# Gather, scatter and their place in the expert loop of a two-layer decoder step

## The reference, cut to what matters

```python
logits = (h @ w_router) + b_router
top_v, top_i = lax.top_k(logits, 2)
top_w = softmax(top_v)
combine = sum(one_hot(top_i, 8) * top_w[..., None], axis=-2)
for e in range(8):
    g, u = split(h @ w_gu[e], 2)          # 1024 -> 2 x 3584
    out += combine[:, e:e+1] * ((silu(g) * u) @ w_down[e])   # 3584 -> 1024
```

## Time and profile before

| what | value |
|---|---|
| three runs | 2363.34, 2367.22, 2367.55 us |
| median | 2367.22 us |
| span of the profiled execution | 2364.9 us (the page gives no other time of it) |
| TensorE busy | 2150.8 us, 91% |
| VectorE busy | 1484.2 us, 63% |
| ScalarE busy | 1091.4 us, 46% |
| mean granted TensorE clock | 0.944 of full |
| read from memory | 533.32 MB, 230 GB/s over the span |

### The profile page before, as it was taken

The page is one execution under the profiler, slowest core; times in us unless marked ns, Lnnn a source line. Parts: engine busy times, 40 slices in busy tenths (PEclk is TensorE's granted clock), DMA queues, the critical chain, the costliest instruction groups (busy, mean ns, idle before and its releaser), DMA issues.

```text
span 2364.9 us, 29561 instructions
## 1 busy us (share of the span) xinstructions
PE 2150.8 (91%) x10775; PEld 1662.0 (70%) x10775; DVE 1484.2 (63%) x1684; ACT 1091.4 (46%) x961; POOL 14.9 (1%) x26
## 2 busy tenths in 40 slices
PE   5989899869877899998978999999999999999995
PEld 2443355545656699997966878788787878788783
DVE  5980220267331444535567979788887979788885
ACT  4740020024220233333324757676676757676672
POOL 0000100000000000000000000000000000000000
PEclk9999999957988999998987999999999999999997
DMA  9984333200354564453425979899797979899790
GB/s 320 386 296 110 116 111 114 83 1 1 114 157 121 223 240 160 164 174 110 143 73 176 371 288 368 317 329 373 283 368 284 367 289 373 313 329 373 279 371 25
DMA packets 262788, 537.62 MB, mean 227 GB/s; under 512 B 14876, under 2 KB 56068, under 8 KB 262438
## 3 DMA queue, kind: packets, MB, share of 16 engines
q1 hardware_dynamic: 258514, 520.34, 62.6%
q0 software_dynamic: 1984, 13.45, 1.7%
q10 hardware_dynamic: 2196, 2.61, 0.3%
HBM read 533.32 MB, written 11.35 MB: 230 GB/s over the span
## 4 chain that ended last, share of the span: by engine, by line
PE 85%; DVE 9%; ACT 3%; issue 2%; DMA 1%; ACTq 1%; DVEq 0%; POOL 0%; PEldq 0%
PE ps L1358 23%; PE ps L1846 13%; PE ps L1825 9%; PE ps L1827 9%; PE ps L1826 9%; PE ps L1684 5%; PE ps L1686 5%; PE ps L1685 5%; DVE alo L798 2%; PE ps L1574 1%; PE ps L1486 1%; DMA ring<-in_w_ada 1%; PE ps L1809 1%; ACT ahi L593 1%; PE ps L1589 1%
## 5 line engine op out<-in xcount | busy, mean ns | idle before, releaser
L1307 DVE TENSOR_TENSOR wlo<-ring,whi 128x2048 fp32r<-128x2048 f32 x336 | 767.1, 2290 | 118.0 <-ACT whi L757 118.0
L757 ACT ACTIVATE whi<-ring 128x2048 fp32r<-128x2048 f32 x336 | 642.1, 1918 | 232.9 <-PE ps L1827 166.3
L1825 PE MATMUL ps<-whi,XTh 128*128 128x512 f32 x896 | 355.2, 396 | 0.0
L1827 PE MATMUL ps<-whi,XTl 128*128 128x512 f32 x896 | 350.0, 391 | 0.0
L1826 PE MATMUL ps<-wlo,XTh 128*128 128x512 f32 x896 | 349.3, 390 | 0.0
L1825 PEld LDWEIGHTS ps<-whi,XTh 128*128 128x128 f32 x896 | 168.6, 188 | 36.1 <-DVE wlo L1307 2.5
L1827 PEld LDWEIGHTS ps<-whi,XTl 128*128 128x128 f32 x896 | 168.5, 188 | 36.0
L1826 PEld LDWEIGHTS ps<-wlo,XTh 128*128 128x128 f32 x896 | 168.8, 188 | 33.5
L1150 DVE TENSOR_TENSOR flo<-ring,fhi 128x2048 fp32r<-128x2048 f32 x42 | 96.3, 2292 | 137.4 <-ACT fhi L600 137.4
L600 ACT ACTIVATE fhi<-ring 128x2048 fp32r<-128x2048 f32 x42 | 80.6, 1920 | 174.0 <-PE ps L1686 174.0
L1684 PE MATMUL ps<-hTh,fhi 128*128 128x288 f32 x448 | 132.5, 296 | 10.3 <-DVE hTl L1159 10.3
(11 more groups left out here) (321 smaller groups left out, 3271.4 us busy)
## 6 DMA issues: line engine op xcount, KB each, us to landing
ring<-in_w_moe_gu SPq DMA_DIRECT2D x224, 1024.0 KB, 7.0
ring<-in_w_moe_down SPq DMA_DIRECT2D x112, 1024.0 KB, 7.0
ring<-in_w_ada SPq DMA_DIRECT2D x48, 1024.0 KB, 10.4
ring<-in_w_ff_gu SPq DMA_DIRECT2D x28, 1024.0 KB, 5.2
ring<-in_cache_cmp_kv SPq DMA_DIRECT2D x128, 128.0 KB, 2.1
ring<-in_cache_sel_kv SPq DMA_DIRECT2D x128, 128.0 KB, 2.1
ring<-in_w_ff_down SPq DMA_DIRECT2D x14, 1024.0 KB, 5.1
ring<-in_w_conv_in SPq DMA_DIRECT2D x12, 1024.0 KB, 5.1
```

What stands on the lines that cost most here:

```text
L757: a.activation(whi[:, i % SPLIT, :], ring[:, (T_MOE + i) % RING, :], ACT.Copy).then_inc(s_split_hi, 1)
L1307: v.tensor_tensor(wlo[:, i % SPLIT, :], ring[:, (T_MOE + i) % RING, :], whi[:, i % SPLIT, :].bitcast(F32), ALU.subtract).then_inc(s_used, 1)
L1825: pe.matmul(out, XTh[:, kc, :], hi, start=kc == 0, stop=False)
L1827: ins = pe.matmul(out, XTl[:, kc, :], hi, start=False, stop=kc == 7)
```

## The change

The gather takes two steps. `hN` is kept as two rounded halves: ScalarE rounds the rows to `hNh`, VectorE makes the rest `hNl`. The one-hot `Dm` is now the stationary operand and the rows are the moving one, 512 columns at a time: 2 halves of the width by 3 token tiles by 2 row halves, 12 fp32r matmuls, into banks 2 and 3. ScalarE copies that to `actM`, TensorE turns it by 8 transposes into banks 0 and 1, and ScalarE and VectorE split it into `XTh` and `XTl` as before.

The scatter uses a plain one-hot: `DT` is now "weight greater than 0", and the weight of each slot (`slotw`, the sum over tokens of the turned `Dw`) is multiplied into y when y is rounded to `ysh` (ScalarE, with a scale operand) and `ysl` (VectorE). So the scatter is 8 chunks of two fp32r matmuls of 288 columns. There is one buffer for half of y, so the second half of y is rounded after the first four chunks.

The place changes too. The scatter of expert e runs in the stream of expert e+1: one chunk after each of the gate and up tiles 0 to 3 and 6 to 9. The turning of `Dw` comes after tile 11, and the making of `DT`, `slotw` and the next matrices on VectorE after the split of tile 13. The gather for the next expert stands before down tile 7 and its turning before down tile 9. The last expert does a gather as well, which nobody uses, and its scatter follows the loop. Before the first expert a gather stands alone, and `ps` banks 6 and 7, `slotw` and `DT` are cleared, so that the first scatter in the loop adds zeros. The buffers get places of their own, and the output rows `outN` no longer share `hN`.

```diff
@@ ScalarE
+            def gathered(g):
+                for h in range(2):
+                    a.wait_ge(s_gathered, g * 2 + (h + 1))
+                    a.activation(actM[:, h, :], ps[:, 2 + h, :], ACT.Copy).then_inc(s_xg_ready, 1)
+
+            def gathered_hi(g):
+                for h in range(2):
+                    a.wait_ge(s_xg_turned, g * 2 + (h + 1))
+                    a.activation(XTh[:, 4 * h:4 * h + 4, :], ps[:, h, :].rearrange("p (c s) -> p c s", c=4),
+                                 ACT.Copy).then_inc(s_xt_hi, 1)
+
+            def y_hi(h):
+                a.activation(ysh[:], ps[:, 6 + h, :], ACT.Identity, scale=slotw).then_inc(s_y_hi, 1)
+
+            for i in range(6):
+                a.wait_ge(s_rows_done, i + 1)
...
+                a.activation(hNh[0:m, t, 512 * h:512 * h + 512], ps[0:m, i, :], ACT.Copy).then_inc(s_rows_hi, 1)
...
+                a.wait_ge(s_round_clear, rnd + 1)
+                y_hi(0)
+                gathered(B)
+                gathered_hi(B)
                 with a.Fori(0, NE) as e0:
...
+                        if i == 5:
+                            a.wait_ge(s_share_done, (e0 + B) * 8 + 4)
+                            y_hi(1)
+                        if i == 36:
+                            gathered(e0 + (B + 1))
+                        if i == 38:
+                            gathered_hi(e0 + (B + 1))
...
                     a.wait_ge(s_tile_done, e * TILES_E + (SPLIT_AT_M + TILES_E))
-                    a.activation(ysb[:, 0:512], ps[:, 6, :], ACT.Copy).then_inc(s_y_act, 1)
+                    a.wait_ge(s_scatter_ready, e + 1)
+                    y_hi(0)
+                a.wait_ge(s_share_done, (B + NE) * 8 + 4)
+                y_hi(1)
@@ VectorE
+            def add_share(g, c):
+                v.wait_ge(s_share_done, g * 8 + (c + 1))
+                v.tensor_tensor(yacc[:, c, :], yacc[:, c, :], ps[:, 6 if c < 4 else 6 + c % 2, 0:NTOK], ALU.add
+                                ).then_inc(s_share_added, 1)
+
+            def y_lo(g, h):
+                v.wait_ge(s_y_hi, g * 2 + (h + 1))
+                v.scalar_tensor_tensor(out=ysl[:], in0=ps[:, 6 + h, :], scalar=slotw, in1=ysh[:].bitcast(F32),
+                                       op0=ALU.mult, op1=ALU.subtract).then_inc(s_y_lo, 1)
...
+                v.memset(ps[:, 6:8, :], 0.0)
+                v.memset(slotw, 0.0)
+                v.memset(DT[:].bitcast(F32), 0.0).then_inc(s_round_clear, 1)
                 matrices(rnd, 0, base)
+                y_lo(B, 0)
+                gathered_lo(B)
                 with v.Fori(0, NE) as e0:
...
+                        if 2 <= i <= 5:
+                            add_share(e0 + B, i - 2)
+                        if i == 5:
+                            y_lo(e0 + B, 1)
+                        if 8 <= i <= 11:
+                            add_share(e0 + B, i - 4)
+                        if i == 13:
+                            v.wait_ge(s_weights_turned, e + 1)
+                            v.tensor_scalar(DT[:], ps[:, 7, 0:NTOK], 0.0, None, ALU.is_gt)
+                            v.tensor_reduce(slotw, ps[:, 7, 0:NTOK], AX, ALU.add).then_inc(s_scatter_ready, 1)
                             matrices(rnd, e0 + 1, e0 * L + (base + L))
+                        if i == 38:
+                            gathered_lo(e0 + (B + 1))
...
+                    y_lo(e0 + (B + 1), 0)
@@ TensorE
+            def gather(g):
+                pe.wait_ge(s_gather_ready, g + 1)
+                for h in range(2):
+                    for t, (_, m) in enumerate(TOK):
+                        for k, part in enumerate((hNh, hNl)):
+                            ins = pe.matmul(ps[:, 2 + h, :], Dm[0:m, t, :], part[0:m, t, 512 * h:512 * h + 512],
+                                            start=t == 0 and k == 0, stop=t == 2 and k == 1)
+                    ins.then_inc(s_gathered, 1)
+
+            def turn_gathered(g):
+                for h in range(2):
+                    pe.wait_ge(s_xg_ready, g * 2 + (h + 1))
+                    for c in range(4):
+                        ins = pe.transpose(ps[:, h, 128 * c:128 * c + 128], actM[:, h, 128 * c:128 * c + 128], ident)
+                    ins.then_inc(s_xg_turned, 1)
+
+            def share(g, c):
+                if c % 4 == 0:
+                    pe.wait_ge(s_y_lo, g * 2 + (c // 4 + 1))
+                if c:
+                    pe.wait_ge(s_share_added, g * 8 + (c if c < 5 else c - 1))
+                out = ps[:, 6 if c < 4 else 6 + c % 2, 0:NTOK]
+                pe.matmul(out, ysh[:, 128 * (c % 4):128 * (c % 4) + 128], DT[:], start=True, stop=False)
+                pe.matmul(out, ysl[:, 128 * (c % 4):128 * (c % 4) + 128], DT[:], start=False, stop=True).then_inc(s_share_done, 1)
...
+                gather(B)
+                turn_gathered(B)
                 with pe.Fori(0, NE) as e0:
...
                                 if kc % 4 == 3:
                                     ins.then_inc(s_tile_done, 1)
+                                    if i < 4:
+                                        share(e0 + B, i)
+                                    if 6 <= i < 10:
+                                        share(e0 + B, i - 2)
+                                    if i == 11:
+                                        pe.wait_ge(s_share_added, (e0 + B) * 8 + 8)
+                                        for t, (t0, m) in enumerate(TOK):
+                                            ins = pe.transpose(ps[:, 7, t0:t0 + m], Dw[0:m, t, :], ident[0:m, 0:m])
+                                        ins.then_inc(s_weights_turned, 1)
...
+                        if i == 7:
+                            gather(e0 + (B + 1))
+                        if i == 9:
+                            turn_gathered(e0 + (B + 1))
...
+                for c in range(DC):
+                    share(B + NE, c)
+                pe.wait_ge(s_share_added, 8 * (B + NE + 1))
```

More of the change, by code:

```diff
@@ L91, in trunk, with moe_sb @@
         oT = hT
+        moe_ctx = ExitStack()
+        def moe_sb(name, shape, dt=F32R):
+            return moe_ctx.enter_context(nc.sbuf_tensor(name, shape, dt))
+        ysh = moe_sb("ysh", [128, 512])
+        ysl = moe_sb("ysl", [128, 512])
+        Dm = moe_sb("Dm", [128, 3, 128])
+        DT = moe_sb("DT", [128, NTOK])
+        Dw = moe_sb("Dw", [128, 3, 128], F32)
+        moe_ctx.close()
         nT = sb("nT", [128, DC, NTOK])
@@ L160, in trunk @@
         conv_ctx.close()
-        hN = sb("hN", [128, 3, D])
+        out_ctx = ExitStack()
+        outN = out_ctx.enter_context(nc.sbuf_tensor("outN", [128, 3, D], F32))
+        out_ctx.close()
+        hNh = sb("hNh", [128, 3, D], F32R)
+        hNl = sb("hNl", [128, 3, D], F32R)
         XTh = sb("XTh", [128, DC, 128], F32R)
@@ L216, in trunk @@
         yacc = hT
[L217 to L222, removed]
         nine = route[:, 0:81]
@@ L344, in trunk @@
         s_rows_taken = sem("s_rows_taken")
+        s_rows_hi = sem("s_rows_hi")
         s_gathered = sem("s_gathered")
+        s_xg_ready = sem("s_xg_ready")
+        s_xg_turned = sem("s_xg_turned")
         s_split_hi = sem("s_split_hi")
@@ L1293, in matrices, with gathered_lo @@
                 for t in range(3):
-                    ins = v.tensor_scalar(Dw[:, t, :], Dm[:, t, :], cur[:, 2, t:t + 1], None, ALU.mult)
+                    ins = v.tensor_scalar(Dw[:, t, :], Dm[:, t, :].bitcast(F32), cur[:, 2, t:t + 1], None, ALU.mult)
                 ins.then_inc(s_gather_ready, 1)
+            def gathered_lo(g):
+                for h in range(2):
+                    v.wait_ge(s_xt_hi, g * 2 + (h + 1))
+                    v.tensor_tensor(XTl[:, 4 * h:4 * h + 4, :], ps[:, h, :].rearrange("p (c s) -> p c s", c=4),
+                                    XTh[:, 4 * h:4 * h + 4, :].bitcast(F32), ALU.subtract).then_inc(s_xt_lo, 1)
+            def add_share(g, c):
[6 more added lines that the diff above has]
+                                       op0=ALU.mult, op1=ALU.subtract).then_inc(s_y_lo, 1)
             def experts(rnd):
                 L = 3 if rnd else 2
+                B = (NE + 1) * rnd
                 base = {0: 0, 1: 18, 2: 45}[rnd]
@@ L1328, in experts @@
                                             actTh[:, 4 * j:4 * j + 4, :].bitcast(F32), ALU.subtract).then_inc(s_eactT_lo, 1)
[L1329 to L1334, removed]
+                    y_lo(e0 + (B + 1), 0)
+                for c in range(DC):
+                    if c == 4:
+                        y_lo(B + NE, 1)
+                    add_share(B + NE, c)
+                v.wait_ge(s_share_added, 8 * (B + NE + 1))
             experts(0)
@@ L1848, in experts @@
                         ins.then_inc(s_tile_done, 1)
-                    pe.wait_ge(s_y_act, e + 1)
-                    pe.wait_ge(s_y_dve, e + 1)
-                    for c in range(DC):
-                        if c >= 4:
-                            pe.wait_ge(s_share_added, e * 8 + (c - 3))
```

(5 more changed lines are left out.)

25 lines of the change are left out of this document (13 added, 12 removed).

## The result

The changed kernel took 2395.75 us (median of 4 runs, 2395.61 to 2396.83) beside 2365.48 us (median of 4, 2363.34 to 2367.55) for the kernel before: a ratio of 1.0126, 95% interval 1.0109 to 1.0142. It is slower by about 30 us, where I forecast 12.6. The profiled execution's span grew from 2364.9 to 2393.6 us, +28.7, and the mean granted TensorE clock fell from 0.944 to 0.932.

The account below looks back on a forecast made before the run. TensorE was taken to bound the kernel, with 15.15 us per expert boundary on its path. Boundaries +3.5, last expert +7.5, tail +3.2 and start -1.6 gave +12.6 us, 2380 on the median 2367.2; range 2358 to 2393.

Parts of the forecast that it names:

- a boundary's net: Per expert boundary: -8.65 removed, +6.2 TensorE stream, +1.65 clock, +1.3 stalls, so +0.5 us; seven give +3.5.
- The sign that I had set for being wrong: An expert's period under 132.5 or over 135.5 us, above all by the clock or VectorE's burst.
- step 1: Expert boundary: 6.5 us stays of 15.15, as ScalarE rounds y before the next first tile; removal worth 8.65 us.
- step 2: Gather 2.75, turning back 0.72, scatter 2.13 and weights' transposes enter TensorE's stream: 6.2 us per expert.
- step 4: Stalls after the boundary: tile 7 about 0.4 us late, VectorE's burst delays tiles 14 and 15; 1.3 us together.
- step 3: TensorE's pause at each boundary drops its clock to the lower level for 3.5 us: 1.65 us lost, bounds 0 to 3.3.
- step 6: Tail behind the last expert: 8.9 us instead of 5.65, with 0.95 per early share: +3.2 us.
- step 7: Start: first gather about 5 instead of 15.1 us, expert 0 begins at 1268.1 instead of 1269.7: -1.6 us.
- A: Rival: the clock holds at 2.4 GHz through the boundary pause, worth 7 x 1.65; 2368 us, chance 0.07.
- B: Rival: both ScalarE table loads of an expert vanish, worth 12 us; 2368 us, chance 0.08.
- C: Rival: VectorE's burst and tile 7 are covered, no stall, 8 x 1.3 less; 2369 us, chance 0.10.
- D: Rival: VectorE's steps cost their full durations and the low clock lasts 5 us; 2391 us, chance 0.16.

Follow-up runs that it names:

- e2_rows: The changed kernel with the gather's third token tile widened from 32 to 128 rows, the extra rows zero: 2382.50 us, 1.0073 of the kernel before.
- e1_warm: The changed kernel with 24 idle matmuls behind each expert's last down tile to fill TensorE's pause: 2382.43 us, 1.0072 of the kernel before.
- e7_burst: The changed kernel with the next expert's one-hot matrices made on VectorE behind tile 19, not 13: 2387.83 us, 1.0092 of the kernel before.
- e3_table: The changed kernel with one tiny silu, its result never read, ahead of the experts' loop: 2378.37 us, 1.0052 of the kernel before.
- e4_heads: The changed kernel with the next expert's first tile halves made before and around the rounding of y: 2329.32 us, 0.9847 of the kernel before.
- e6_back: The changed kernel with all eight scatter chunks back ahead of the next expert's first gate tile: 2404.76 us, 1.0165 of the kernel before.

## Why the prediction came out as it did

The side was right, slower; the size was not: 28.7 us of span against 12.6, and the measured time lies above the range. No new wait turned up that the sum lacked. Four of its terms were too small, and it counted because a boundary's net was the small difference of two large numbers, -8.65 and +9.15, so an error of a tenth in either is larger than the net of 0.5. The sign that I had set for being wrong, a period under 132.5 or over 135.5, was too wide for this: the mean period of 135.22 lies inside it, and yet seven times its distance from the forecast's 133.6 is 11 us.

**The boundary that stays (step 1): right.** 6.57 against 6.5, with y_hi at 0.69 against 0.70 and the load at 1.28. That the removal is worth 8.6 us holds.

**TensorE's stream (step 2): mis-sized, +8.2 us with step 4.** The gather's 12 passes, 2.75 us forecast, took 3.46, and 0.16 more in the tile behind: 0.87 short, 7.0 us in eight experts and the largest single error. The step that failed is "each a twelfth of a tile, 0.229": it priced by columns alone, and the 32-row passes among 128-row ones start 0.32 to 0.34 apart. e2_rows shows it. The earlier trace rows gave no warning, since its 48 passes are one group. The transposes took 0.90 instead of 0.72, the shares 2.28 instead of 2.13. "Nothing there" for the wait at the gather was right.

**The clock (step 3): mechanism right, size +4.4 us.** 2.28 us per boundary instead of 1.65: the low clock lasted 2.9 to 6.2 us behind the seven pauses, by the granted clock of the trace, mean about 4.9, not 3.5. I took the mean of the two stretches of the earlier trace rows; with two samples the spread of seven could not be seen. e1_warm confirms the price, which lies within the bounds of 0 and 3.3.

**The stalls (step 4): right in sum.** Tile 7 cost about 0.27 more than before, tiles 13 to 15 0.88; together 1.15 against 1.3. The burst's part falls on tile 14 (0.68), where I had 0.2 for it and 0.7 for tile 15. e7_burst and e3_table took them away one by one.

**The tail (step 6): mis-sized by 2.15 us.** I put a share with its add and back at 0.95. TensorE in the tail of the changed kernel, the first four shares (its last slot ended at 2344.63):

```profile
2346.36 0.40 PE L1881 MATMUL ps<-DT,ysh 128*128 128x288 f32 x1 [1.56 <-DVE ysl L1355]
2347.44 0.41 PE L1881 MATMUL ps<-DT,ysh 128*128 128x288 f32 x1 [0.55 <-DVE hT L1350]
2348.64 0.61 PE L1881 MATMUL ps<-DT,ysh 128*128 128x288 f32 x1 [0.55 <-DVE hT L1350]
2350.03 0.61 PE L1881 MATMUL ps<-DT,ysh 128*128 128x288 f32 x1 [0.55 <-DVE hT L1350]
```

The steps are 1.08, then 1.20 and 1.39. The first is already above my 0.95, at the full clock; then the clock fell here too (0.64 in the mean of the tail), and I had reckoned the tail at full clock.

**The start (step 7): mis-sized by 1.5 us.** The gather of expert 0 took 6.3 us at the low clock, not about 5, again by its unequal rows, and nothing was won.

**The rivals.** A (the clock holds) fell with the granted clock of 0.50 at every boundary; e1_warm shows what it would have been worth, 16 us at the boundaries. B (the table loads go) didn't happen by itself; e3_table shows that it is to be had for one instruction: 17 us by the medians, of which some 14 can be tied to the loads, against my 12. C fell with the stalls of 1.15. D was nearest, 2391 against a measured 2395.75, but for half of its reason: the low clock lasted its 5 us, while VectorE's steps cost what I had. Left out was a rival in which the gather's unequal passes cost more than their columns.

## What to carry to other kernels

Work that is moved out of a serial stretch into the stream of the engine that bounds still costs its time there; it pays only by what the stretch gets shorter. So first ask what the stretch waits for once it is empty, here two halves of a tile behind a rounding, and put that ahead of the wait. The same moved work was worth +30 us with a 6.4 us pause left (the changed kernel), and -36 us with the pause closed (e4_heads). No run puts that order, or the one silu, into the kernel before. Where a forecast is a difference of two large terms, price each group by a row of its own shape, and give the clock's return its spread.

## What the runs showed of the hardware that I had not expected

- Matmuls of equal columns start 0.32 to 0.34 us apart instead of 0.23 where 128 and 32 rows of contraction alternate. Multiplying 96 rows of zeros is faster (2.80 against 3.46 us for twelve).
- After pauses of equal length (6.4 us) the low clock lasted from 2.9 to 6.2 us in the changed kernel, where the periods differ by 1.5 us. In e3_table, where they agree within 0.12, it lasted 4.2 to 4.3 us each time (pause 5.0). What sets it in one case was not settled, nor how short a pause keeps the clock: 5.0 us loses it, 0.81 us (e1_warm) and 1.0 (the kernel before) keep it. Between lie only the chains of shares in e6_back and in the tail, 1.6 us of pause and then steps about half idle, in which it fell.
- The table load at a loop's head depended on what ran before the loop. One activation of eight columns took two loads out of every expert; the run was 17 us faster, some 14 of them by the loads.
